# Small vectors requested by ScalarE in the first stage, store waits of SP put where their data is first used, and semaphores cleared by POOL

## The reference

```python
def reference(x, c, ctx, c_ctx, ada_w, ..., w_out_2):
    x = first_block(x, c, ctx, c_ctx, ada_w, ada_b, norm1_g, w_in, ...)
    return second_block(x, c_2, ctx_2, c_ctx_2, norm_g_2, w_mod_2, ...)

# first_block, cut
sh1, sc1, g1, sh2, sc2, g2 = split(silu(c) @ ada_w + ada_b)   # and the same of c_ctx
p = modulate(rmsnorm(x), sh1, sc1) @ w_in                     # and pc of ctx
filt = hyena_filter_freqs(...)                                # sine network, window, real FFT
y_hy = hyena_mixer(p[..., :3 * HY_WIDTH], filt)               # two long convolutions
y_hg = hgrn_mixer(p[..., 3 * HY_WIDTH:], pc, ...)             # gated scan, both directions
x = x + g1 * (concat(rmsnorm(y_hy), y_hg) @ w_out)
x = x + g2 * ec_moe(modulate(rmsnorm(x), sh2, sc2))           # 16 experts, each its top 128 tokens
x = rmsnorm(x, final_g)
# second_block: two layers of a mixer
#   p = (modulated norm of x) @ w_in; Fourier mix, pooled mix and differential attention over
#   its columns; x = x + gate * ((concatenation * silu(g)) @ w_out)
```

## Time and profile before

| | |
|---|---|
| executions | 4079.36, 4081.03, 4086.21 us |
| median | 4081.03 us |
| profiled execution | 4076.85 us, its span 4075.1 us |
| busy share of the span | PE 91%, DVE 63%, ACT 47%, POOL 20% |
| instructions | 44172 |
| transferred | 779 MB, 191 GB/s over the span |

### The profile page before, as it was taken

How to read it: one execution, slowest core, us unless ns; L and a number is a source line. 1 busy time by engine, 2 the same in 40 slices (tenths; PEclk the granted TensorE clock), 3 DMA queues, 4 the chain that set the end, 5 groups by cost and what they waited for, 6 DMA issues and landing times. The chain is left out here.

```text
span 4075.1 us, 44172 instructions
## 1 busy us (share of the span) xinstructions
PE 3715.1 (91%) x17357; PEld 2889.7 (71%) x17357; DVE 2573.2 (63%) x2795; ACT 1898.4 (47%) x2499; POOL 799.7 (20%) x591
## 2 busy tenths in 40 slices
PE   7999898986778899999999998999898899998988
PEld 4887644446667388887878786778777577787857
DVE  5445364548956888888888887651376625515753
ACT  5211200047654376777777676451266314514731
POOL 2100034210012002121212111420144224202422
PEclk9999898998888999999999998999999999999999
DMA  5553315111043899999999998443420433435123
GB/s 193 203 181 128 113 67 189 54 69 45 27 151 146 291 368 369 383 368 376 370 379 365 372 379 287 142 130 115 172 94 14 156 125 120 135 108 198 52 93 119
DMA packets 389065, 779.10 MB, mean 191 GB/s; under 512 B 26168, under 2 KB 110003, under 8 KB 388600
## 3 DMA queue, kind: packets, MB, share of 16 engines
q1 hardware_dynamic: 366074, 699.46, 47.9%
q0 software_dynamic: 17856, 66.33, 4.9%
q10 hardware_dynamic: 4928, 10.49, 0.8%
HBM read 664.74 MB, written 111.48 MB: 190 GB/s over the span
## 5 line engine op out<-in xcount | busy, mean ns | idle before, releaser
L3012 DVE TENSOR_TENSOR moe_w_low<-shared_z,moe_w_high 128x2048 fp32r<-128x2048 f32 x256 | 594.0, 2365 | 92.7 <-ACT moe_w_high L2965 91.3
L2965 ACT ACTIVATE moe_w_high<-shared_z 128x2048 fp32r<-128x2048 f32 x256 | 476.8, 1914 | 175.4 <-DMA shared_z<-in_exp_w 168.7
L172 PE MATMUL moe_bank<-moe_w_high,moe_xgT_high 128*128 128x512 f32 x1024 | 404.5, 395 | 10.9 <-DVE moe_w_low L3012 5.9
L174 PE MATMUL moe_bank<-moe_w_high,moe_xgT_low 128*128 128x512 f32 x1024 | 399.9, 391 | 0.0
L173 PE MATMUL moe_bank<-moe_w_low,moe_xgT_high 128*128 128x512 f32 x1024 | 399.8, 390 | 0.0
L3012 DVE TENSOR_TENSOR moe_w_low<-moe_w_raw,moe_w_high 128x2048 fp32r<-128x2048 f32 x128 | 287.3, 2286 | 62.3 <-ACT moe_w_high L2965 61.7
L2965 ACT ACTIVATE moe_w_high<-moe_w_raw 128x2048 fp32r<-128x2048 f32 x128 | 238.3, 1910 | 116.4 <-DMA moe_w_raw<-in_exp_w 115.2
L3238 POOL TENSOR_SCALAR layer_att_p<-layer_att_p,layer_att_rinv,layer_att_neg_lam 128x1280 f32<-128x1280 f32 (+1 forms) x72 | 173.4, 2408 | 527.2 <-DVE layer_att_neg_lam L3267 313.4
L3245 DVE TENSOR_REDUCE layer_att_nb<-layer_att_scores 128x1 f32<-128x1280 f32 (+1 forms) x144 | 195.0, 1369 | 88.8 <-PE layer_att_scores L3150 87.7
L172 PE MATMUL layer_front_bank<-layer_front_w_high,layer_front_hT_high 128*128 128x512 f32 (+1 forms) x608 | 229.6, 378 | 7.9 <-POOL layer_front_hT_low L799 7.9
L172 PEld LDWEIGHTS moe_bank<-moe_w_high,moe_xgT_high 128*128 128x128 f32 x1024 | 192.9, 188 | 56.2 <-DVE moe_w_low L3012 9.9
(11 more groups left out here) (556 smaller groups left out, 8574.7 us busy)
## 6 DMA issues: line engine op xcount, KB each, us to landing
shared_z<-in_exp_w SPq DMA_DIRECT2D x128, 2048.0 KB, 10.3
moe_w_raw<-in_exp_w SPq DMA_DIRECT2D x64, 2048.0 KB, 10.3
shared_z<-in_w_in SPq DMA_DIRECT2D x48, 512.0 KB, 6.5
first_raw<-in_w_in SPq DMA_DIRECT2D x32, 512.0 KB, 7.5
front_vec<-in_ada_w POOLq DMA_DIRECT2D x16, 1024.0 KB, 5.9
late_raw<-in_w_mod SPq DMA_DIRECT2D x8, 2048.0 KB, 8.3
proj_t<-front_out SPq DMA_DIRECT2D x48, 256.0 KB, 2.2
shared_z<-in_w_out SPq DMA_DIRECT2D x12, 1024.0 KB, 6.1
```

Source lines behind the costliest of these rows:

```text
L172: nc.tensor.matmul(out, lhs[0], rhs[0], start=start, stop=False)
L174: return nc.tensor.matmul(out, lhs[1], rhs[0], start=False, stop=stop)
L2965: nc.scalar.activation(hi, x, ACT.Copy).then_inc(high, 1)
L3012: nc.vector.tensor_tensor(lo, x, hi.bitcast(F32), ALU.subtract).then_inc(low, 1)
```

## The change

In `mods` the identity, the vectors and the bias are requested by ScalarE, as the first instructions of its list; SP requests the weights at once, in eight halves of 1 MB, each with a semaphore of its own, and ScalarE waits for each half. The clearing of retired semaphores stands at the head of POOL's list in every block. The waits for stores at the end of five blocks (three fronts, `filter`, `hgrn`) are removed; a new helper, `stored`, waits for the same semaphores at the first use: SP in `filter` as its first instruction, ScalarE in `hyena` ahead of the first spectra loads, SP in `mixout` behind the second weight request, SP in `layer_att` as its first instruction. The last scatter of the experts is issued by POOL in the first layer's front, behind the clears. In `filter` the two tables are given their place in memory first.

```diff
--- before.py
+++ after.py
@@ -91,6 +91,11 @@
     def sem(self, name):
         return self.stack.enter_context(self.nc.semaphore(name))
 
+    def stored(self, eng, lanes):
+
+        for lane in lanes:
+            eng.wait_ge(lane.sem, lane.at(0))
+
     def dram(self, name, shape, dt=F32):
         kind = "ExternalOutput" if self.tap and name in self.tap else "Internal"
         return self.nc.dram_tensor(name, shape, dt, kind=kind).ap()
@@ -140,10 +145,10 @@
         with self.nc.Block() as block:
             retired, core.retired_sems = core.retired_sems, mine
             if retired:
-                @block.sync
-                def _(sp):
+                @block.gpsimd
+                def _(pool):
                     for s in retired:
-                        sp.sem_clear(s)
+                        pool.sem_clear(s)
             yield block
         core.zeroed_sems += retired
 
@@ -225,14 +230,11 @@
         with st.block() as block:
             @block.sync
             def _(sp):
-                sp.dma_start(core.ident[:, :], io["t_ident"]).then_inc(vecs, 16)
-                for dst, src in loads:
-                    sp.dma_start(dst, src).then_inc(vecs, 16)
-                sp.dma_start(bias[:, :], io["ada_b"][0][0:nc_].partition_broadcast(2)).then_inc(biases, 16)
                 for i, (name, l, g) in enumerate(groups):
-                    sp.dma_start(raw[i][:, :, :],
-                                 io[name][l, :, g * BANK:(g + 1) * BANK].rearrange("(k p) n -> p k n", p=P)
-                                 ).then_inc(core.load[i].sem, 16)
+                    for s, c in enumerate(halves):
+                        sp.dma_start(raw[i][:, c, :],
+                                     io[name][l, c.start * P:c.stop * P, g * BANK:(g + 1) * BANK].rearrange(
+                                         "(k p) n -> p k n", p=P)).then_inc(core.load[8 * s + i].sem, 16)
                 ahead_w(sp)
                 for i in range(2):
                     sp.wait_ge(low, 2 * i + 2)
@@ -270,6 +272,10 @@
 
             @block.scalar
             def _(act):
+                act.dma_start(core.ident[:, :], io["t_ident"]).then_inc(vecs, 16)
+                for dst, src in loads:
+                    act.dma_start(dst, src).then_inc(vecs, 16)
+                act.dma_start(bias[:, :], io["ada_b"][0][0:nc_].partition_broadcast(2)).then_inc(biases, 16)
                 act.wait_ge(cols_copied, 1)
                 core.act(act, nc.scalar.activation(silu_all[:, :], core.col_a[:, 0:32], ACT.Silu))
                 nc.scalar.activation(silu.high[:, :], silu_all[:, :], ACT.Copy).then_inc(silu_done, 1)
@@ -277,10 +283,10 @@
                 nc.scalar.activation(lbe[:, :, :], lbd[:, :, :], ACT.Exp).then_inc(mods_done, 1)
 
                 for i in range(len(groups)):
-                    act.wait_ge(core.load[i].sem, core.load[i].at(1))
                     if i >= RP:
                         act.wait_ge(w_used, i - RP + 1)
-                    for c in halves:
+                    for s, c in enumerate(halves):
+                        act.wait_ge(core.load[8 * s + i].sem, core.load[8 * s + i].at(1))
                         nc.scalar.activation(w[i % RP].high[:, c, :], raw[i][:, c, :], ACT.Copy).then_inc(high, 1)
 
             @block.vector
@@ -328,6 +334,7 @@
                                                                  core.col_a[:, g:g + 8], ALU.add, ALU.mult))
         for i in range(RING):
             core.load[i].close(1)
+            core.load[8 + i].close(1)
 
 
 LATE = [(l, g) for l in range(2) for g in range(6)]
@@ -784,10 +791,6 @@
                         for v, dst in enumerate((core.k_high, core.k_low) if which else (core.q_parts,)):
                             sp.dma_start(dst[:, :, col].rearrange("h p t -> p h t"), staged[c % 2][v][:, :, :].bitcast(F32)
                                          ).then_inc(core.hstore[RS + c % 2].sem, 16)
-                for j in range(RS):
-                    sp.wait_ge(core.hstore[j].sem, core.hstore[j].at(len(range(j, len(plain), RS))))
-                for j in range(2 if R else 0):
-                    sp.wait_ge(core.hstore[RS + j].sem, core.hstore[RS + j].at(stores_of(j, R)))
 
             @block.gpsimd
             def _(pool):
@@ -840,6 +843,8 @@
 
                 if vectors:
                     sums.fill_pick(pool)
+                if space:
+                    core.last_scatter(pool)
                 for i in range(-2, N + 4):
                     if 0 <= i + 2 < n:
                         low_of(i + 2)
@@ -1258,10 +1263,10 @@
     with Stage(core, name) as st:
         st.sb("inputs", [P, KD * BANK + 4 * D])
         win, wave, w_in, skip = core.filter_in
+        tab = [st.sb("cos", [P, NT, SEQ // 2]), st.sb("sin", [P, NT, SEQ // 2])]
         wave_high, hs = st.sb("wave_high", [P, SEQ], F32R), st.sb("hs", [P, SEQ], F32R)
         w_fold = st.sb("w_fold", [P, 2, 2, HY])
         w_high, w_low = (st.sb(k, [P, 2, 2, HY], F32R) for k in ("w_high", "w_low"))
-        tab = [st.sb("cos", [P, NT, SEQ // 2]), st.sb("sin", [P, NT, SEQ // 2])]
         lag0 = st.sb("lag0", [P, 2])
         fold = [[st.sb(f"sum{o}", [P, NT, HY]), st.sb(f"dif{o}", [P, NT, HY])] for o in range(2)]
         whole, first = [st.sb(f"abs{i}", [P, 2, HY]) for i in range(2)], [st.sb(f"first{i}", [P, HY]) for i in range(2)]
@@ -1282,6 +1287,7 @@
         with st.block() as block:
             @block.sync
             def _(sp):
+                core.stored(sp, core.hstore[0:6])
                 sp.dma_start(lag0[:, :], io["t_lag0"]).then_inc(windows, 16)
                 sp.dma_start(tab[0][:, :, :], io["t_lag_cos"].rearrange("(j p) k -> p j k", p=P)).then_inc(tables, 16)
                 sp.dma_start(tab[1][:, :, :], io["t_lag_sin"].rearrange("(j p) k -> p j k", p=P)).then_inc(tables, 16)
@@ -1300,8 +1306,6 @@
                         row = (f + m * HF) * P
                         sp.dma_start(core.spectra[o, s, row:row + P, :], out[n % RS][:, :]
                                      ).then_inc(core.hstore[n % RS].sem, 16)
-                for j in range(RS):
-                    sp.wait_ge(core.hstore[j].sem, core.hstore[j].at(len(range(j, 2 * len(pairs), RS))))
 
             @block.tensor
             def _(pe):
@@ -1648,6 +1652,7 @@
                     if o == 0:
                         place_u(0)
                         place_u(1)
+                        core.stored(act, core.hstore[0:6])
                         for f in range(RSP):
                             act.dma_start(spec[f][:, :, :], core.spectra[0, :, f * P:(f + 1) * P, :].rearrange(
                                 "s p c -> p s c")).then_inc(core.load[4 + f].sem, 16)
@@ -2001,8 +2006,6 @@
                             sp.dma_start(out_g, core.vg[0:P, BANK:2 * BANK]).then_inc(core.load[2].sem, 16)
                             sp.wait_ge(core.hstore[0].sem, core.hstore[0].at((H - 1) * NT // 4 + 1))
                             sp.dma_start(out_o, core.hg_o[0:P, :].rearrange("p (h c) -> p h c", c=P)).then_inc(core.load[0].sem, 16)
-                for j in range(4):
-                    sp.wait_ge(core.hstore[j].sem, core.hstore[j].at(H * NT // 4))
 
             @block.scalar
             def _(act):
@@ -2443,6 +2446,7 @@
                 load_w(0)
                 load_hyena(0, 2, hyena)
                 load_w(1)
+                core.stored(sp, core.hstore[0:4])
                 tile(1)
                 sp.dma_start(gate[:, :], core.mod_rows[0][0, 2 * D:3 * D].partition_broadcast(P)).then_inc(gain, 16)
                 residual(0)
@@ -2823,6 +2827,14 @@
         g2 = st.sb("g2", [P, D])
         bank = st.banks(8)
         gathered, scattered = st.dma_sem("gathered"), core.scattered
+
+        def last_scatter(pool):
+            pool.wait_ge(scattered, 16 * (E - 1))
+            pool.indirect_dma_start(out=core.x1, out_offset=bass.IndirectOffsetOnAxis(
+                ap=core.moe_idx[:, E - 1:E], axis=0), in_=yo[(E - 1) % 2][:, :], in_offset=None,
+                compute_op=ALU.add).then_inc(scattered, 16)
+
+        core.last_scatter = last_scatter
         (high, low, xwhole, gain, w_used, xturn, xplaced, silu, hidden, hturn, hhigh, hplaced, yout) = (
             st.sem(k) for k in ("high", "low", "x_whole", "gain", "w_used", "x_turned", "x_placed", "silu", "hidden",
                                 "h_turned", "h_high", "h_placed", "y_out"))
@@ -2879,7 +2891,6 @@
                         scatter(e - 1)
                     if e + 1 < E:
                         split_x(e + 1)
-                scatter(E - 1)
 
             @block.tensor
             def _(pe):
@@ -3119,6 +3130,7 @@
                         for dst, src in ((q_parts, core.q_parts), (k_high, core.k_high), (k_low, core.k_low)):
                             sp.dma_start(dst[h % 2][:, m, :].bitcast(F32), src[2 * h + m, :, :]).then_inc(lane.sem, 16)
 
+                core.stored(sp, core.hstore[0:8])
```

## The result

The changed kernel took 4058.55 us (median of 4054.84 to 4061.42) against 4083.06 us of the kernel before beside it: 0.9941 of it, with a 95% interval of 0.9925 to 0.9956. Compared twice more, it came to 0.9949 (0.9937 to 0.9961) and 0.9945 (0.9931 to 0.9959). The mean of the three is a gain of 0.55%, some 22 us. The forecast was 4066.8 us, a gain of 14.2, in a range of 4058 to 4080.

The account below looks back on a forecast made before the run. TensorE, busy 91% of the span, was taken as the bound, leaving 360 us to move, mostly in untouched stages. Terms for first stage, waits, clears and scatter summed to 14.2 us: 4081.0 to 4066.8 us, range 4058 to 4080.

Parts of the forecast that it names:

- First stage: Kernel start, `mods`: weights requested at once by SP, vectors by ScalarE; first product earlier, gain 1.5 us (−1.2 to 3.6).
- V: Time at which the first stage's vectors have landed, taken as 10.6 us; first products start near 8.0 us after it.
- Rival (a): First stage: vectors served only behind all SP's weights, losing 10.9 us there; whole kernel 4079.2 us; chance 0.13.
- its sign of 13 us: First stage: transposes later than 13 us would show that the vectors stand behind the weights.
- front to filters: End of first front stage: store wait moved into the filter block, gain 1.4 us; POOL's later zeros cost 0 to 1.5.
- Filters to hyena: End of filter block: store wait moved and SP freed of 18 clears, gain 2.6 us (1.5 to 3).
- Scan to projection: End of scan stage: store wait moved and 20 clears off SP before the output projection, gain 2.2 us (1.1 to 2.5).
- The two fronts: Ends of the two front stages ahead of attention: store waits moved, gains 1.4 and 1.7 us, at least 1.2 each.
- The clears: Semaphore clears moved from SP to POOL: scan start gains 1.2 us; experts' gather loses 0.8, mixers 1.0 each.
- The mixers' −2.0: Two mixer block starts: 14 clears delay POOL's last fill, which releases TensorE; loss 1.0 us in each.
- The scatter: End of experts' block: barrier 8.0 us earlier, less about 3 of stall for the first tile; gain 5.0 (3 to 6.4).
- rival (d): Block starts: clears dear on POOL, kernel slower from 0.25 us a clear, 4093 us at 0.4; chance 0.04.

## Why the prediction was right, and which of its terms were not

The direction held, and so did the mechanism of the two largest groups of terms, the waits and the scatter. The range held barely: 4058.55 us lies 0.55 us above its lower end, and the gain (24.5 us in that comparison, 21 and 22.5 in the two later ones) is above the 20 us to which all good ends add up, so only the 3 us allowed for the scatter of runs took it in. That the total came out inside is in part luck, since the first stage and the clears were sized wrong in opposite directions. By the forecast's own steps:

- **First stage**, forecast 1.5 us gained in bounds of −1.2 to 3.6: measured about −0.4. The pace of the requests was nearly right (0.39 us each against 0.43 assumed). The middle of the sum had a slip: by the rule of its two bounds, 22 requests at 0.43 make V 11.1 and the gain 1.0, not 10.6 and 1.5. The step that failed is the landing: V was 12.8 to 13.0 us, since I added 0.9 us for it from the undisturbed rows, and beside SP's weights it was 4.3. The rest of the chain was 7.8 us against 8.0. Rival (a), with the vectors behind all the weights, didn't happen, though its sign of 13 us was all but reached: they landed at 13.00 when three of the eight halves were there (the third at 12.35) and SP was still issuing. The Trainium skill's "DMA: Bandwidth & Descriptors", section "Issuing engines are not separate DMA queues", has it that a second issuing engine saves the issuing time only. The trace agrees: nothing beyond the 7.2 us of issuing was won, and here the loss among the weights took back even that.
- **The waits**: front to filters 1.4, measured 1.4 (the block went from 424.52 to 423.08 us). Filters to hyena 2.6, measured 1.5 to 1.7 at the end and 1.1 behind the barrier. Scan to projection 2.2, measured 1.3 at the barrier and 1.1 behind it. The two fronts 1.4 and 1.7: the second block is 2.1 us shorter, the first 0.9, in which the scatter's stall is contained.
- **The clears**, forecast +1.2 at the scan and −2.8 elsewhere: the scan gave 1.5. The gather cost nothing: it was issued 0.8 us later and landed at the same place (6.0 to 6.9 us behind the barrier in all traces), so that its landing is not set by its issue alone. The mixers' −2.0 did not come. I had read TensorE's release by POOL and not VectorE's, which waits for the later of a table that SP requests behind its clears and a load of POOL's, and starts up to 1.7 us earlier; the two mixers stayed as long as they were (145.0 against 145.2 us, but for one trace). At the router I had put nothing, where SP's late weights come some 1.3 us earlier. On the other side, I had put nothing at the output blocks, where the first product is 0.65 us later, twice (below). By these steps, with 1.1 at the hyena block and 1.1 at the projection, the clears give 3.7 us, and 6 to 8 by the timing, where their share of the forecast was 0.5 (with 1.0 and 1.1 at those two): the largest part of what the forecast fell short by.
- **The scatter**, forecast 5.0 in bounds of 3 to 6.4: 8 us at the barrier as forecast, with a stall of 0.7 to 2.2 us where I took about 3. The timing gives 2 to 5 us; the traces give 3.3 for the scatter alone and about 7 in the changed kernel; the forecast lies between.
- **Slower by dear clears**, rival (d): 0.07 us on POOL as assumed, against the 0.25 from which it decides.

The steps read from the traces give about 18 us, as do the block means (17), against 22 timed. The remaining 4 us have no step of their own. What goes along with them is TensorE's granted clock: its mean was 0.9602 and 0.9610 over the 12 and 15 executions of the kernel before, and 0.9640 and 0.9626 over the six and five of the changed kernel beside them. Among 56 timed executions of the kernel before, 0.001 more of it goes with 1.6 us less time; at that rate (an estimate) 3 to 6 us of the gain go with the clock. That is an association: no run shows what raised the clock, or that it is the cause.

## What to carry to other kernels

An instruction at the head of a queue costs what stands behind it on that queue, so look at every consumer of the block's first loads on both engines: the mixers showed TensorE starting 1 us later, VectorE earlier, and the blocks as long as before. A wait belongs where its data is used, and a transfer whose landing only a drain waits for can go behind the barrier if its reader comes late. Requests that a chain hangs on should be through before large loads begin on any queue: splitting them over two engines and putting the weights behind them won 6 to 7 us, where putting them beside the weights won nothing.

## What the runs showed of the hardware that was not expected

A small request of ScalarE landed 1.4 us after its issue with no large load ahead of it, and 4.3 us after with SP's 1 MB loads in flight. The last indirect scatter, of 512 KB, landed 6.0 to 8.2 us after its issue over the fourteen traces, the 15 ahead of it, beside the experts' weights, 8.7 to 11.3. The latest of the last scatters were those of the two kernels in which POOL issued it behind the barrier without clears ahead of it: 7.4 and 8.2 us. The earlier issue won them nothing.

VectorE's first split in the output blocks became slower beside work of POOL's. The changed kernel's first split beside POOL's subtraction, and below it that of the kernel in which SP clears there:

```profile
3221.96 1.27 POOL L3694 TENSOR_TENSOR layer_out_y_low<-layer_y_y_att,layer_out_y_high 128x512 fp32r<-128x512 f32 x1
3222.36 5.23 DVE L3672 TENSOR_TENSOR layer_out_w_low<-shared_z,layer_out_w_high 128x2048 fp32r<-128x2048 f32 x2 [3.28 <-ACT layer_out_w_high L3649]
```

```profile
3219.19 1.26 POOL L3696 TENSOR_TENSOR layer_out_y_low<-layer_y_y_att,layer_out_y_high 128x512 fp32r<-128x512 f32 x1
3220.24 4.57 DVE L3674 TENSOR_TENSOR layer_out_w_low<-shared_z,layer_out_w_high 128x2048 fp32r<-128x2048 f32 x2 [3.28 <-ACT layer_out_w_high L3651]
```

POOL is 0.65 us later against the barrier, VectorE is not; the two overlap for 0.9 us instead of 0.2, and VectorE's two splits take 5.23 us instead of 4.57. It is the first of them that grows, 3.02 us against 2.37, at both outputs, in all fourteen traces, according to whether POOL or SP clears there. So a delay on POOL that no instruction waits for cost 0.65 us at each of the two outputs.
